# Expert stage in full fp32: 64-token blocks in two column groups, each expert's weights loaded once, half-row gathers

## What is computed

```python
def routed_experts(h2d, idx, gw, w_gate, w_up, w_down):
    ...
    def expert_block(args):
        xb, e = args
        hb = jax.nn.silu(xb @ w_gate[e]) * (xb @ w_up[e])
        return hb @ w_down[e]
    out = lax.map(expert_block, (buf.reshape(n_blocks, MOE_BLOCK, d), block_expert))
    contrib = out[dest] * g_sorted[:, None].astype(out.dtype)
    return jnp.zeros((t, d), h2d.dtype).at[tok_sorted].add(contrib)

h = modulate(rms_norm(x, norm2_w), sh2, sc2).reshape(bsz * seq, d)
idx, gw = grouped_route(h, w_router, router_bias)
y = routed_experts(h, idx, gw, w_gate, w_up, w_down).reshape(bsz, seq, d)
return x + g2[:, None, :] * y
```

## Time and profile before

| | us |
|---|---|
| median of the runs | 3037.66 (3035.31 to 3037.86, 3 runs) |
| span of the profiled execution | 3041.9 |
| first matmul of the expert stage | 1651.0 |
| last down matmuls begin | 2988.5 |

### The profile page before, as it was taken

One profiled execution on the slowest core, in us unless ns is written; L12 is line 12 of the kernel. 1 busy time (PEld: TensorE's weight loads), 2 busy tenths in 40 slices (PEclk: granted clock), 3 DMA queues, 4 the chain that ended last, 5 costly groups with the idle time before them and its releaser, 6 DMA issues.

```text
span 3041.9 us, 34857 instructions
## 1 busy us (share of the span) xinstructions
PE 2759.4 (91%) x12582; PEld 2240.1 (74%) x12582; DVE 2356.1 (77%) x1894; ACT 1565.1 (51%) x1510; POOL 548.3 (18%) x432
## 2 busy tenths in 40 slices
PE   2799999999999788999965999999999999999992
PEld 2577777777677566788864888778888877887872
DVE  4879989987857575444445999889999888988894
ACT  6322222222122653333323877777888777777773
POOL 0000000000211110100001333222343222423230
PEclk8899999999999698999986999999999999999996
DMA  9733333334856426555536899999999999999997
GB/s 326 264 111 104 97 104 97 104 104 132 277 187 198 156 80 233 176 190 181 203 97 240 348 374 365 361 378 375 384 368 372 381 377 378 373 373 369 371 388 278
DMA packets 243520, 781.30 MB, mean 257 GB/s; under 512 B 27713, under 2 KB 122065, under 8 KB 173949
## 3 DMA queue, kind: packets, MB, share of 16 engines
q1 hardware_dynamic: 198738, 615.29, 53.0%
q0 software_dynamic: 34144, 130.08, 14.0%
q10 hardware_dynamic: 10570, 35.05, 3.0%
HBM read 738.30 MB, written 87.11 MB: 271 GB/s over the span
## 4 chain that ended last, share of the span: by engine, by line
PE 31%; DMA 12%; DVE 7%; SPq 5%; issue 4%; ACT 3%; DVEq 0%; POOL 0%; ACTq 0%; POOLq 0%
DMA wraw<-in_w_up_dram 8%; SPq L1514 4%; PE ps L1572 4%; PE ps L1570 4%; PE ps L1571 4%; PE ps L1768 3%; PE ps L1770 3%; PE ps L1769 3%; DVE wlo L1590 3%; PE ps L1870 2%; PE ps L1871 2%; PE ps L1875 2%; ACT whi L1580 2%; DMA wraw_o<-in_w_out_dram 2%; PE ps L1559 1%
## 5 line engine op out<-in xcount | busy, mean ns | idle before, releaser
L1590 DVE TENSOR_TENSOR wlo<-wraw,whi 128x2048 fp32r<-128x2048 f32 x444 | 1003.7, 2285 | 101.9 <-ACT whi L1580 101.6
L1580 ACT ACTIVATE whi<-wraw 128x2048 fp32r<-128x2048 f32 x444 | 848.2, 1918 | 311.5 <-PE ps L1572 91.3
L1570 PE MATMUL ps<-whi,xhi 128*128 128x512 f32 x1184 | 476.7, 403 | 4.5 <-DVE wlo L1590 4.4
L1572 PE MATMUL ps<-whi,xlo 128*128 128x512 f32 x1184 | 464.6, 392 | 0.0
L1571 PE MATMUL ps<-wlo,xhi 128*128 128x512 f32 x1184 | 462.9, 391 | 0.0
L715 PE MATMUL ps<-hh,wih 128*128 128x512 f32 x1056 | 336.9, 400 | 6.3 <-DVE wil L703 6.3
L715 PE MATMUL ps<-hl,wih 128*128 128x512 f32 x1056 | 330.4, 394 | 0.0
L715 PE MATMUL ps<-hh,wil 128*128 128x512 f32 x1056 | 329.9, 393 | 0.0
L1049 DVE SCALAR_TENSOR_TENSOR acc<-u,vcur,acc 128x1024 f32<-128x1024 f32 x240 | 308.3, 1284 | 8.0
L1570 PEld LDWEIGHTS ps<-whi,xhi 128*128 128x128 f32 x1184 | 224.1, 189 | 49.7 <-DVE wlo L1590 7.5
L1572 PEld LDWEIGHTS ps<-whi,xlo 128*128 128x128 f32 x1184 | 222.8, 188 | 48.6
(11 more groups left out here) (375 smaller groups left out, 4300.8 us busy)
## 6 DMA issues: line engine op xcount, KB each, us to landing
wraw<-in_w_gate_dram SPq DMA_DIRECT2D x148, 1024.0 KB, 8.5
wraw<-in_w_up_dram SPq DMA_DIRECT2D x148, 1024.0 KB, 11.8
wraw<-in_w_down_dram SPq DMA_DIRECT2D x148, 1024.0 KB, 10.9
wm<-in_w_mod_dram POOLq DMA_DIRECT2D x88, 512.0 KB, 4.1
wraw_i<-in_w_in_dram SPq DMA_DIRECT2D x72, 512.0 KB, 4.7
wraw_o<-in_w_out_dram SPq DMA_DIRECT2D x128, 256.0 KB, 3.5
wmA<-in_w_mod_dram SPq DMA_DIRECT2D x54, 512.0 KB, 5.4
u<-in_w_mod_dram POOLq DMA_DIRECT2D x24, 512.0 KB, 4.6
```

The costliest lines, as they stand in the source:

```text
L1570: pe.matmul(dst, xhi[:, t, :], whi[:, s, w], start=(t == 0), stop=False)
L1572: last = pe.matmul(dst, xlo[:, t, :], whi[:, s, w], start=False, stop=(t == KT - 1))
L1580: act.activation(whi[:, spl(m), :], wraw[:, raw(m), :], ACT.Copy).then_inc(s_whi, 1)
L1590: dve.tensor_tensor(wlo[:, spl(m), :], wraw[:, raw(m), :], whi[:, spl(m), :].bitcast(F32), ALU.subtract).then_inc(s_wsp[raw(m)], 1)
```

## The change

**Blocks and weights.** The block becomes 64 tokens (`BLK = 64`), which makes 49 blocks for these inputs, 22 experts with one block, six with two, two with three, one with four, one with five. The loop over items becomes a loop over experts, with an inner loop over the blocks of that expert, whose bounds TensorE reads from DRAM. The experts are visited in the order `visit(o) = o % 8 * 4 + o // 8`; the numbers of blocks in that order are 1 1 2 1 1 3 1 2 1 2 1 1 1 5 1 1 1 1 2 1 1 4 1 1 1 1 2 1 1 3 1 2. Each expert's 12 pieces are loaded once. Gate and up have room for two experts (`ring`, 16 slots), down for one (`dring`, 4 slots). The pieces are used where they land.

**Arithmetic.** No rounding and no splitting: the matmuls are plain fp32. A block has 64 rows, so the stationary operand is 64 columns wide. The up product goes to PSUM partitions 0 to 63 and the gate product to 64 to 127, in turn; the down product has its first 1024 columns in the lower and its last 1024 in the upper half. In one block TensorE has 32 matmuls of 64x512 for gate and up, 16 for down, and 12 transposes.

**Rows.** A token row is fetched as two half rows of 4 KiB, into 128 partitions by 1024; the output is stored the same way. ScalarE has one instruction in a block (silu), VectorE five.

**Order of loads.** SyncE no longer reads an expert's number, since the order of visits is fixed; it reads one count for each expert. The first expert's eight gate and up pieces are issued with no wait for the stores of `h2_d`, and down and half of the second expert's gate and up are issued before the table `items_d` is stored.

The heart of the diff, with parts left out. The loop over `o` is SyncE's. In `block_of`, which is TensorE's, the transposes of the hidden values and the down product are those of block j - 1, and the transposed rows are those of block j + 1:

```diff
-BLK = 128
+BLK = 64
+            def visit(o):
+                return o % G * EG + o // G
+            def gu_slot(o, m):
+                return m // 4 * 8 + m % 4 + 4 * ((o + 1) % 2)
...
-                def round_w(act, i, m, last=False):
-                    act.wait_ge(s_we[raw(m)], 16 * raw_turn(i, m) + 16)
-                    ...
-                    act.activation(whi[:, spl(m), :], wraw[:, raw(m), :], ACT.Copy).then_inc(s_whi, 1)
-                def split_w(dve, i, m, last=False):
-                    ...
-                    dve.tensor_tensor(wlo[:, spl(m), :], wraw[:, raw(m), :], whi[:, spl(m), :].bitcast(F32),
-                                      ALU.subtract).then_inc(s_wsp[raw(m)], 1)
+                def gate_up(pe, j, par, v):
+                    pe.wait_ge(s_hb, j + 1)
+                    for q in range(4):
+                        if q % 2 == 0:
+                            pe.wait_ge(s_xT, 2 * j + q // 2 + 1)
+                        for kind in (UP, GATE):
+                            pe.wait_ge(s_wg[2 * q + kind], 16 * v)
+                        for k in range(4):
+                            h, t = k_tile(q, k)
+                            for kind in (UP, GATE):
+                                rows_ = slice(0, BLK) if kind == UP else slice(BLK, 2 * BLK)
+                                last = pe.matmul(ps[rows_, BANK_GU:BANK_GU + FE], xT[:, t, h, :],
+                                                 ring[:, gu_slot(par, 2 * q + kind), FE * k:FE * k + FE],
+                                                 start=(q + k == 0), stop=(q + k == 6))
+                        last.then_inc(s_guq[q], 1)
+                def down(pe, v):
+                    for t in range(FT):
+                        pe.wait_ge(s_wd[t], 16 * v)
+                        for n in range(2):
+                            for half in range(2):
+                                c0 = HALF_ROW * half + 512 * n
+                                last = pe.matmul(ps[BLK * half:BLK * half + BLK, BANK_D + 512 * n:BANK_D + 512 * n + 512],
+                                                 hidT[:, t, :], dring[:, t, c0:c0 + 512], start=(t == 0), stop=(t == FT - 1))
+                        last.then_inc(s_dt[t], 1)
...
+                    for o in range(1, E):
+                        through = blocks_through(sp, o - 1)
+                        if o + 1 < E:
+                            for m in range(8):
+                                if m % 2 == 0:
+                                    sp.wait_ge(s_guq[m // 2], through)
+                                load_gate_up(sp, o + 1, m)
+                        for t in range(FT):
+                            sp.wait_ge(s_dt[t], through + 1)
+                            load_down(sp, o, t)
...
+                    def block_of(j, par, v):
+                        gate_up(pe, j, par, v)
+                        transpose_hidden(pe)
+                        pe.wait_ge(s_xr2, 16 * j + 32)
+                        transpose_rows(pe)
+                        w = turn(pe, j)
+                        pe.wait_ge(s_hT, j + 1)
+                        pe.wait_ge(s_or, j + 1)
+                        down(pe, w)         
+                    with pe.Fori(0, E // 2) as a:
+                        for par in range(2):
+                            with pe.Fori(blocks_before(pe, 2 * a + par), blocks_through(pe, 2 * a + par)) as j:
+                                block_of(j, par, 2 * a + par + 1)
```

More of the change, by code:

```diff
@@ L1516, in raw, with turn, blocks_before @@
[L1516 to L1528 removed]
+            def turn(eng, i):
+                return eng.value_load(items_d[ds(i, 1), 0:1], min_val=1, max_val=E)
+            def blocks_before(eng, o):
+                return eng.value_load(nitems_d[0:1, ds(2 + o, 1)], min_val=0, max_val=MAX_ITEMS)
@@ new lines, in transpose_rows, with transpose_hidden @@
+                def transpose_rows(pe):
+                    v = xrow[:].rearrange("p (c t) -> p t c", t=KT // 2)
+                    for t in range(KT // 2):
+                        last = pe.transpose(ps[:, BANK_X + t * P:BANK_X + (t + 1) * P], v[:, t, :], ident[:])
+                        if t % 4 == 3:
+                            last.then_inc(s_xt2, 1)
+                def transpose_hidden(pe):
+                    v = hb[0:BLK, :].rearrange("p (m t) -> p t m", t=FT)
+                    for t in range(FT):
+                        last = pe.transpose(ps[:, BANK_H + t * BLK:BANK_H + (t + 1) * BLK], v[:, t, :], ident[0:BLK, 0:BLK])
+                    last.then_inc(s_hbt, 1)
@@ L1640, in _ @@
                         sp.dma_start(gp[:, 1024 * h:1024 * h + 1024], src).then_inc(s_gp, 16)
+                    for j in range(HT, TT):
+                        sp.wait_ge(s_h2s[j], 16)
+                    for t in range(FT):
+                        load_down(sp, 0, t)
+                    sp.wait_ge(s_hs, 3 * HT)
+                    for j in range(HT, TT):
+                        sp.wait_ge(s_x1[j], 16)
+                    for m in range(4):
+                        load_gate_up(sp, 1, m)
                     sp.wait_ge(s_tab, 1)
@@ L1822, in _ @@
                     pe.wait_ge(s_gws, 1)
-                    for q in range(4):
-                        last = pe.matmul(ps[:, 1024 + 512 * q:1536 + 512 * q], ones[:], gp[:, 512 * q:512 * q + 512],
-                                         start=True, stop=True)
+                    pe.wait_ge(s_ls, 2)
+                    for n in range(2):
+                        for half in range(2):
+                            c0 = HALF_ROW * half + 512 * n
+                            last = pe.matmul(ps[BLK * half:BLK * half + BLK, BANK_G2 + 512 * n:BANK_G2 + 512 * n + 512],
+                                             ones[:, 0:BLK], gp[:, c0:c0 + 512], start=True, stop=True)
@@ L1881, in _ @@
-                    with pe.Fori(0, n_items) as i:
-                        work(i)
-                    work(n_items, last=True)
+                    transpose_rows(pe)
[3 more added lines that the diff above has]
+                        pe.wait_ge(s_xr2, 16 * j + 32)
+                        transpose_rows(pe)
+                        w = turn(pe, j)
+                        pe.wait_ge(s_hT, j + 1)
+                        pe.wait_ge(s_or, j + 1)
+                        down(pe, w)
@@ L1885, in _ @@
+                    pe.wait_ge(s_hT, n_items + 2)
+                    pe.wait_ge(s_or, n_items + 2)
+                    down(pe, w)
                 @block.scalar
@@ new lines, in rows_out, with hidden @@
+                    def rows_out(j):
+                        for a in range(2):
+                            dve.wait_ge(s_xt2, 2 * j + a + 1)
+                            dve.tensor_copy(xT[:, 4 * a:4 * a + 4, :, :].rearrange("p t h r -> p (t h r)"),
+                                            ps[:, BANK_X + 512 * a:BANK_X + 512 * a + 512]).then_inc(s_xT, 1)
+                    def hidden(j):
+                        dve.wait_ge(s_gs, j + 1)
+                        dve.tensor_tensor(hb[0:BLK, :], ps[0:BLK, BANK_GU:BANK_GU + FE], gsl[0:BLK, :], ALU.mult).then_inc(s_hb, 1)
@@ L2384, in _ @@
+                    dve.memset(hb[0:BLK, :], 0.0).then_inc(s_hb, 1)
+                    dve.memset(orow[:], 0.0).then_inc(s_or, 2)
+                    rows_out(0)
+                    hidden_out(0)
+                    rows_out(1)
+                    hidden(0)
                     dve.wait_ge(s_g2, 2)
                     with dve.Fori(0, n_items) as i:
-                        work(i)
-                    work(n_items, last=True)
+                        hidden_out(i + 1)
+                        rows_out(i + 2)
+                        hidden(i + 1)
+                        out_rows(i)
```

407 lines of the change are left out of this document (125 added, 282 removed).

## The result

The changed kernel takes 3190.9 us (median of 4 runs, 3175.8 to 3210.3) against 3037.8 us for the kernel before on the same chip: a ratio of 1.050, 95% interval 1.045 to 1.054. It is 5% slower where 2.2% faster was forecast. The time lies in the range of 2900 to 3270 us, on the other side of it. The profiled execution has a span of 3174.0 us. The ratios in this document leave out two executions that lie far from the others of their kernel, 11017 us (one of four in experiment 1) and 3239.9 us (one of thirteen of the kernel before), and no run shows what made them long.

The account below looks back on a forecast made before the run. The expert stage was taken as bound by TensorE and, nearly as much, by weight loads. Start 1664, stage 1260 (1170 work, 80 stalls, 10 clock) and end 51 gave 2975, less 4 for 2971 us; range 2900 to 3270.

Parts of the forecast that it names:

- The step that failed: TensorE at each expert's start: idle time left by two double DRAM reads, taken as 1.5 us, 48 us in all.
- the stock: TensorE's queue of matmuls issued ahead, 4.0 us, behind which its DRAM reads hide.
- the reads of DRAM show in full: Rival: TensorE's queue drains at each wait, a block takes 26.5 us, an expert's start 7.8, in all 3260; chance 0.12.
- Clock and stalls for weights: Expert stage: 10 us for lower clock after stalls in a dozen dry experts, 80 us of waits for late weights.
- the reserve model: Weight loads over the visits: a reserve loaded ahead, capped at 20 or 10 us, gives stalls of 55 or 99 us.
- The block: TensorE's work for one block: gate/up 14.0, down 7.0, transposes 1.6, read ahead of down 0.3, together 22.9 us.
- The overlap of the column groups: Gate/up and down matmuls: the array's two halves work side by side, each 0.43 us slot holding two records.
- the rival of 0.52 to 0.62: Rival: the halves overlap only in part, slots grow from 0.43 to 0.52 to 0.62 us, in all 3143; chance 0.17.
- The weights' rate: Weight loads in the expert stage: 0.408 MB/us, so an expert's twelve pieces take 30.8 us.
- the row path: Gathering and storing token rows: 14 to 18 us for each block, hidden under the block's 22.9 us.
- The read ahead of down: TensorE's double DRAM read before each down: 1.4 to 3.9 us, hidden but for 0.3 us a block.
- The start: Before the expert stage: more pieces queued ahead of small tables delay the first matmul by 13 us, to 1664.

Follow-up runs that it names:

- experiment 1: Changed kernel with TensorE's loops over experts and blocks written out with constants, so it reads no DRAM in the stage; 2939.9 us, ratio 0.965.
- experiment 3: Changed kernel with every weight load cut to its first 512 columns, a quarter of the bytes, DRAM reads kept; 2891.9 us.
- experiment 5: Changed kernel with the gate product on the same half of the array's columns as up, in another bank; 3820.7 us.
- experiment 10: From version 2, the table of owners that TensorE reads ahead of each down also built as a row in SBUF; 2937.7 us, ratio 0.967.
- version 2: Changed kernel with TensorE's two counts at each expert's start read from SBUF in place of DRAM; 2964.6 us, ratio 0.975.

## Why the prediction went wrong

**The step that failed** is "At each expert's start there are two double reads, 2.8 to 7.8 us, against 4.0 us of stock: 0 to 3.9 us show, I take 1.5." Measured are 8.0 us on average (248.9 / 31), up to 13.3. Three things were wrong in it, in order of size.

- *The duration.* The upper bound was SyncE's median in the kernel before, 3.9 us a double read the earlier trace rows; TensorE's are 6.1 and 4.1 us by the medians here, with single pairs of up to 7.5. SyncE's own maxima, 4434 and 3627 ns, stood in the earlier trace rows and would have given 16 us for two. A median of reads at any moment was taken as a bound for reads that fall where a freed ring is being refilled. That the moment matters is argued from the 411 GB/s in the gap above, against 285 in the stage's mean; that traffic matters is shown by experiment 3. The Trainium skill (DMA: Bandwidth & Descriptors, Latency and other measured facts) gives an HBM access 0.2 us on average and 2 us at high load; the direction agrees, with a pointer load of 1.3 us at its shortest and 4.3 at the median in one line of the kernel after (1527).
- *What stands around it.* Register operations and the way from the last load to the first matmul, 0.89 + 0.86 us in the mean, were costed at nothing, and the stock is 3.35 us, not 4.0. That alone is 2.4 us for each of 31.
- *The value inside the range.* Given 0 to 3.9 us, 1.5 was near the low end, with no row that it was nearest to.

With 8.0 us a start the same sum gives 1260 + 32 x (8.0 - 1.5) = 1468 us of stage, 3179 of time. That this is near 1460.5 and 3191 is in part luck, because two other terms are off the opposite way. The mechanism was among the rivals ("the reads of DRAM show in full", 3260 us, chance 0.12), with 7.8 us a start; but it was tied to a stock that vanishes in every block. The stock is real; the reads outlast it.

**Clock and stalls for weights** were forecast at 10 and 80 us and are 78 and 10 in the trace after. The clock follows from the step that failed: its price of 1.7 us is what a short gap costs (15.06 - 13.36 in experiment 3), but it was set for half a dozen places, and 28 of 31 starts have it. Weights hardly stall an engine that comes this late. Without reads, where the forecast's own picture holds, 136 us (1236.2 - 1100) are 105 us of waits for weights, 22 of clock and 9 of the fiftieth down. So the reserve model was 25 us short. It used a cap of one expert's gate and up and did not count that the first down of an expert with several blocks waits behind the next expert's eight pieces: 54.2 us in 11 waits in experiment 1.

**What held.** The block: 22.9 against 22.45 us. The overlap of the column groups, with its slot of 0.215 us; the rival of 0.52 to 0.62 falls, and experiment 5 shows the factor. The Trainium skill (TensorE: Matmul & The Clock Gate, What overlaps and what doesn't) has weight loads overlap only across row groups; 0.216 us a record with loads of 0.14 us between them, on all rows each time, says otherwise here. The weights' rate: 382.75 MB in 64.0% of 1462 us are 0.409 MB/us (0.408). The end, and the row path, for which TensorE never waited in the stage. The read ahead of down cost 21.7 us in 49 blocks by experiment 10, 0.44 each (0.3). The start at 1662.6 (1664) is right by luck: it holds the four loads of the first expert, for which the trace lists 11.49 us of idle time there and which the forecast had put into the stage; in experiment 1 it is 1651.3.

Version 2, where this one term is taken away, takes 2965 us. The forecast was 2971 with 48 us for that term, so the direction was lost by it; that the two times agree so well is luck again, since version 2 starts its stage 21 us earlier than forecast, and its stage of 1261 has 49 us of other things in place of the 48.

Two slips of the prediction changed nothing: the rate stands at 348 to 388 GB/s in seventeen slices, not eighteen, and 7.8 us less 4.0 are 3.8, not 3.9.

## What to carry to other kernels

A loop whose bounds an engine reads from DRAM costs that engine the read as it is in the worst traffic of the place, plus its register work, less the engine's queued stock; where the value still lies in SBUF, read it there (here 0.39 us against 4 to 6). Price a wait or read by the rows of the same moment, not by a median over a stage, and where a term's range, multiplied by how often it occurs, exceeds the gain that is forecast, that term decides the sign and deserves the most care. Before a load is moved up in a queue, look for what is free to start and will stand behind its wait.

## What the runs showed of the hardware

- A two-step read of DRAM into a TensorE register takes 1.7 us at its best and 6.1 us by the medians of the slower line; with a quarter of the weight traffic that line takes 2.4. The same from SBUF takes 0.30 to 0.49 us in full traffic.
- Two fp32 streams of 64 columns on the two halves of the array run at the full factor of 2 (13.90 against 27.63 us for 64 records), and keep most of it when four matmuls of one half precede four of the other (15.4).
- A gap of 11.5 us left TensorE at 1.2 GHz for the 4 us behind it. In experiment 3, with 2.7 us from the last down matmul to the next gate/up in the mean, 13 of 31 gaps made the gate/up behind them 1.7 us longer or more (15.06 against 13.36 us); in the kernel after 28 of 31 did, by 1.4 to 3.0 us.
